# A second gate buffer for each side of an expert stage, with the residual moved to memory

## What is computed

```python
h = _rmsnorm(x, P['norm_moe_w']) * (1.0 + sc_f) + sh_f
f = _grouped_moe(h.reshape(bsz * L, D_MODEL), router_w, router_bias, ...)
x = x + g_f * f.reshape(bsz, L, D_MODEL)

def _grouped_moe(h, router_w, router_bias, w_gate, w_up, w_down):
    ...   # scores; two of 16 experts for each token; tokens sorted by expert, padded to blocks
    def expert_block(args):
        xb, e = args
        return (jax.nn.silu(xb @ w_gate[e]) * (xb @ w_up[e])) @ w_down[e]
    yb = lax.map(expert_block, (buf.reshape(n_blocks, MOE_BLOCK, D), block_expert)).reshape(n_blocks * MOE_BLOCK, D)
    return jnp.zeros_like(h).at[t_s].add(yb[pos] * w_s[:, None].astype(h.dtype))
```

## Time and profile before

| | us |
|---|---|
| median of 3 runs | 2685.18 |
| profiled execution, its own time | 2692.73 |
| span of its trace | 2690.9 |
| TensorE busy (matmul) | 2516.2 (94%) |
| VectorE busy | 1006.0 |
| ScalarE busy | 709.2 |
| mean granted TensorE clock | 0.981 |

### The profile page before, as it was taken

One profiled execution on the slowest core, in us unless ns is written; L12 is line 12 of the kernel. 1 busy time (PEld: TensorE's weight loads), 2 busy tenths in 40 slices (PEclk: granted clock), 3 DMA queues, 4 the chain that ended last, 5 costly groups with the idle time before them and its releaser, 6 DMA issues.

```text
span 2690.9 us, 39173 instructions
## 1 busy us (share of the span) xinstructions
PE 2516.2 (94%) x16348; PEld 1562.4 (58%) x16348; DVE 1006.0 (37%) x1780; ACT 709.2 (26%) x1252; POOL 66.9 (2%) x66
## 2 busy tenths in 40 slices
PE   6998999999999999999999999999997899989994
PEld 3555888885555566655555556765455444434443
DVE  4356455453223045552342548722345001101115
ACT  3132222221111111120243046731024222222224
POOL 0000000000000000000000000000000000000003
PEclk9999999999999999999999999999998999999997
DMA  7000212204000111141003011131306656657436
GB/s 313 32 32 32 75 47 106 75 31 158 32 32 31 36 52 61 58 162 71 32 18 150 32 38 40 37 118 67 109 21 268 222 209 267 238 229 286 168 135 221
DMA packets 65269, 291.99 MB, mean 109 GB/s; under 512 B 8956, under 2 KB 32068, under 8 KB 44612
## 3 DMA queue, kind: packets, MB, share of 16 engines
q1 hardware_dynamic: 52996, 255.92, 25.2%
q0 software_dynamic: 8928, 22.03, 2.4%
q10 hardware_dynamic: 3168, 11.54, 1.1%
HBM read 694.20 MB, written 56.63 MB: 279 GB/s over the span
## 4 chain that ended last, share of the span: by engine, by line
PE 79%; DMA 8%; DVE 6%; ACT 5%; issue 2%; SPq 1%; POOL 0%; DVEq 0%; ACTq 0%; POOLq 0%
PE psum L531 30%; PE psum L675 15%; PE psum L1519 8%; DMA arena<-in_moe 7%; PE psum L1377 4%; PE psum L1503 4%; PE psum L1102 3%; PE psum L630 2%; ACT arena L1758 2%; PE psum L560 1%; PE psum L1090 1%; PE psum L1015 1%; PE psum L991 1%; PE psum L1488 1%; PE psum L1082 1%
## 5 line engine op out<-in xcount | busy, mean ns | idle before, releaser
L531 PE MATMUL psum<-arena 128*128 128x384 f32 x2544 | 826.8, 487 | 10.9 <-DVEq L330 6.1
L531 PEld LDWEIGHTS psum<-arena 128*128 128x128 f32 x2544 | 483.0, 190 | 352.9 <-issue 10.5
L675 PE MATMUL psum<-arena 128*128 128x384 f32 (+1 forms) x1920 | 541.0, 427 | 6.4 <-ACT arena L689 3.3
L675 PEld LDWEIGHTS psum<-arena 128*128 128x128 f32 x1920 | 341.6, 193 | 155.1 <-issue 6.8
L1519 PE MATMUL psum<-arena 128*32 128x256 f32 x5632 | 325.7, 387 | 31.6 <-DMA arena<-in_moe 30.4
L1519 PEld LDWEIGHTS psum<-arena 128*32 128x32 f32 x5632 | 178.5, 112 | 164.8 <-DMA arena<-in_moe 37.6
L1503 PE MATMUL psum<-arena 128*32 128x512 f32 x1408 | 160.8, 594 | 10.1 <-DMA arena<-in_moe 9.5
L1927 ACT ACTIVATE arena<-psum 32x512 f32<-32x512 f32 x176 | 103.6, 589 | 226.6 <-PE psum L1503 225.0
L1377 PE MATMUL psum<-arena 128*128 128x512 f32 (+1 forms) x384 | 126.0, 487 | 0.3 <-issue 0.3
L2614 DVE TENSOR_TENSOR arena<-arena,psum 128x256 f32<-128x256 f32 x44 | 18.5, 421 | 278.0 <-PE psum L1519 188.1
L689 ACT ACTIVATE arena<-psum 128x384 f32<-128x384 f32 x96 | 46.7, 490 | 277.0 <-PE psum L675 216.7
(11 more groups left out here) (539 smaller groups left out, 2409.6 us busy)
## 6 DMA issues: line engine op xcount, KB each, us to landing
arena<-in_moe SPq DMA_DIRECT2D x532, 1024.0 KB
arena<-in_ada SPq DMA_DIRECT2D x12, 2048.0 KB, 8.8
gate_raw<-arena SPq DMA_DIRECT2D x96, 192.0 KB, 1.8
arena<-gate_raw SPq DMA_DIRECT2D x8, 2304.0 KB, 8.3
y_rows<-arena ACTq DMA_DIRECT2D x22, 512.0 KB
arena<-in_gate SPq DMA_DIRECT2D x5, 2048.0 KB, 8.4
arena<-in_br SPq DMA_DIRECT2D x4, 2048.0 KB, 8.1
arena<-in_qkv SPq DMA_DIRECT2D x3, 2048.0 KB, 15.1
```

The lines of the kernel that those rows point to most:

```text
L531: last = nc.tensor.matmul(pset(s)[:, n, :], w[:, kk, :], src[:, kk, n * N3:(n + 1) * N3], start=(kk == 0), stop=(kk == K - 1))
L675: last = nc.tensor.matmul(bank(6 + u % 2)[:, cols * p:cols * (p + 1)], w[:, m % 4, kk, :], HT[:, kk, n * N3 + cols * p:n * N3 + cols * (p ...
```

## The change

- Each side gets two gate buffers, `gset[i][0]` and `gset[i][1]`, used in even and odd steps. One lies where the gates lay in `wset[i]`, the other where the residual lies (R0 and R0 + 4096).
- The gates of step j + 2 are asked for in iteration j (`gates_ahead`), after the ups of step j + 1 and before the downs of step j. A gate part is one DMA of 2 MB instead of two halves. Whether it is loaded is told by a second table `eint2`, which compares block j with block j − 2. VectorE makes it with two small operations.
- TensorE waits for a step's gates once, on `e_wg[j % 2]`, instead of once for each half.
- The residual is stored in memory (`x_kept`) by nine DMAs of 512 KB in the routing stage (`keep_rows`), in pieces of 128 words. The gates of step 1 are asked for when all nine have landed. After the last gate products nine DMAs bring the rows back to the same place (`x_back`), token by token, and VectorE reads them there.

```diff
+        gset = [[cut(0, 4096), cut(R0, 4096)], [cut(WSET, 4096), cut(R0 + 4096, 4096)]]
+        x_back = [cut(R0 + D * s, D) for s in range(NT)]
...
+            def keep_rows(c0, c1):
+
+                for c in range(c0, c1):
+                    sp.wait_ge(m_htok, 2 * NT + 1 + 2 * (c + 1))
+                    sp.dma_start(x_kept[c * P:(c + 1) * P].rearrange("p (k f) -> p k f", k=KD),
+                                 X[:, :, c * P:(c + 1) * P]).then_inc(s_pstate, 16)
+
+            keep_rows(0, 3)
             sp.wait_ge(m_route, ROUTE_E0)
...
-            for at, done in ((0, e_wg), (4096, e_wu)):
-                for q in range(2):
-                    a = at + 2048 * q
-                    sp.dma_start(wset[1][:, a:a + 2048], first[1][:, a:a + 2048]).then_inc(done[q], 16)
+            sp.dma_start(gset[1][0], first[1][:, 0:4096]).then_inc(e_wg[0], 16)
+            for q in range(2):
+                a = 4096 + 2048 * q
+                sp.dma_start(wset[1][:, a:a + 2048], first[1][:, a:a + 2048]).then_inc(e_wu[q], 16)
+            keep_rows(3, 6)
...
             sp.dma_start(gate_p, grow[0:1].to_broadcast([P, D])).then_inc(m_grow, 16)
+            keep_rows(6, NT)
             sp.wait_ge(m_route, ROUTE_TAB)
+            sp.wait_ge(s_pstate, STATES + 16 * NT)
+            for i in range(2):
+                sp.dma_start(gset[i][1], part_expert(1, i)[:, 0:4096]).then_inc(e_wg[1], 16)
+
+            def gates_ahead(j):
+
+                sp.wait_ge(e_g, 2 * (j - 1))
+                for i in range(2):
+                    at = NST * i + j
+                    e, differs = part_expert(j, i), sp.value_load(eint2[:, at:at + 1], min_val=0, max_val=1)
+                    sp.dma_start(gset[i][j % 2], e[:, 0:4096], cond=(differs > 0)).then_inc(e_wg[j % 2], 16)
...
-                    for at, used, done in ((0, e_g, e_wg), (4096, e_u, e_wu)):
-                        for q in range(2):
-                            sp.wait_ge(used, 2 * j + q + 1)
-                            for i in range(2):
-                                a = at + 2048 * q
-                                sp.dma_start(wset[i][:, a:a + 2048], then[0][i][:, a:a + 2048], cond=(then[1][i] > 0)).then_inc(done[q], 16)
-                if 1 <= j < NST:
+                    for q in range(2):
+                        sp.wait_ge(e_u, 2 * j + q + 1)
+                        for i in range(2):
+                            a = 4096 + 2048 * q
+                            sp.dma_start(wset[i][:, a:a + 2048], then[0][i][:, a:a + 2048], cond=(then[1][i] > 0)).then_inc(e_wu[q], 16)
+                if j + 2 < NST:
+                    gates_ahead(j + 2)
+                if 1 <= j:
                     for q in range(2):
                         sp.wait_ge(e_d, 2 * (j - 1) + q + 1)
...
+            sp.wait_ge(e_g, 2 * NST)
+            for s, c in enumerate(CHUNKS):
+                sp.dma_start(x_back[s], x_kept[c * P:(c + 1) * P]).then_inc(e_wg[0 if s < 4 else 1], 16)
...
-                        pe.wait_ge(ready[q], 32 * (j + 1) + 16)
+                        if w:
+                            pe.wait_ge(e_wu[q], 32 * (j + 1) + 16)
+                        elif q == 0:
+                            pe.wait_ge(e_wg[j % 2], 32 * (j // 2 + 1) + (0 if j % 2 else 16))
...
+            V.then(tt(erow2[:, 2:NB], erow[:, 0, 2:NB], erow[:, 0, 0:NB - 2], ALU.not_equal))
+            V.then(nc.vector.tensor_copy(eint2[:, 2:NB], erow2[:, 2:NB]))
...
-                    xc = X[:, :, c * P:(c + 1) * P]
+                    xc = hd(x_back[s], KD)
```

31 lines of the change are left out of this document (19 added, 12 removed).

## The result

The changed kernel took 2730.19 us, the median of 4 runs from 2721.71 to 2733.17. The kernel before took 2687.45 us beside it, also the median of 4. The ratio is 1.0153, 95% interval 1.0123 to 1.0182: slower, by more than was forecast, and 4 us outside the range.

A forecast was written before the change was run, and what follows sets the result against it. TensorE carried 79% of what ended last, with 44.5 us lost at expert changes. Start 18.5, stage 4 and end 1 gave +23.5: profiled about 2716, less 7.5, predicted 2709 us; range 2688 to 2726, with 62% on 2698 to 2722.

The forecast's parts named there:

- With the single changes: +4: Expert stage: net 13 us saved at single expert changes and 17 lost at dense ones, together 4 us slower.
- the dense changes: Steps 14/15, 19/20, 23/24 and 27/28, expert changes close together: lose 45.4 us against 28.2 before, +17.
- down waits of 5 to 7: Steps 15, 20 and 28: TensorE waits 5 to 7 us for down parts, right behind 2 MB gate transfers.
- The start: Up to step 1: residual stores and both sides' gates delay it to about 2110; +18.5 us, bounds +12 and +22.
- The residual is the trouble: Rival: residual stores and reloads hold the first and last gather, +22 and +3; total 2714, no chance given.
- The end: After the last down product: nine residual reloads run beside the last scatter and first gathers; +1 us, bounds 0 and +3.
- The base: Profiled run taken as 7.5 us above the median of three, 2685.2, so about 2716 became 2709.
- SP kept up: SP's order in the expert stage: four more value loads and moves per iteration, some 2.3 us, would not delay it.
- The bytes: SP's queue: some 32 MB more for gates and 9.4 for the residual.
- Parts overtake: Rival: later transfers pass gates 21 in the queue, downs come in time, only the start is paid; 2668 us, 6%.
- A cheap run: Rival: parts at 0.429 take 4.9 us, stage −7, start at its low end, +12; 2691 us, 17%.
- A slow queue: Rival: long bursts at 356 GB/s, 5.9 us a part, stage +22 and start 18.5; 2726 us, 15%.

The follow-up runs named there:

- single copy: Changed kernel with the second table comparing each block with the one before, so an expert's gates load into one buffer only (some steps compute wrongly): 2697.68 us, ratio 1.0029.
- kept busy: Changed kernel with products of the identity into an unused bank where TensorE waits, at steps 1, 15, 20, 23, 24 and 28: 2727.71 us, ratio 1.0137.
- gate tables early: Changed kernel with SP's value loads for the gates two steps ahead made before its wait for the ups, transfer order unchanged: 2723.49 us, ratio 1.0125.
- gate halves: Changed kernel with each gate part in two 1 MB transfers, first halves of both sides first, and a wait for each half: 2727.03 us, ratio 1.0131.
- no trip: Changed kernel without residual stores and reloads, step 1's gates asked for once the residual is written (output lacks the residual): 2712.88 us, ratio 1.0081.
- the trip alone: Kernel before plus the residual's nine stores and nine reloads, single gate buffer, no wait for the stores before the reload: 2704.05 us, ratio 1.0055.
- Early back: Changed kernel with the nine residual reloads asked for ahead of the last two downs instead of behind them: 2724.93 us, ratio 1.0127.

## Why the forecast was right in direction and too small

**The step that failed** is "With the single changes: +4", the term of the stage, which came out at +15.3, and within it the sum for the dense changes, 45.4 forecast against 53.3 measured, and for the rest, 3.3 against 6.9. The mechanism was as described: more parts in one queue, the downs behind gates not yet needed, down waits of 5.61 at step 20, 5.54 at 28, 2.56 and 0.95 at 15; the single copy shows that the second copies cost 30.5 us where everything else in the stage won 15.1. One sign missed: at 15 down waits of 5 to 7 were forecast. The size was 11.3 us off, and it goes as follows. Step 5 loses 2.0: its gates stand behind the loads for the sample gates, which hold SP until 2139.04 and which the working left out. Steps 8 and 9 lose 1.2 more than worked out. The slow products behind a wait at 20 and 28 make 2.1 to 3.7, by the run that kept TensorE busy; the working took down products at 3.43 us wherever they stood. At 19/20 TensorE in fact waits 8.7 us, less than the 10.5 of the forecast; the other 4.8 of the 13.5 are products that take longer than undisturbed ones, and kept busy shows that most of this time would have been waited for the next part anyway.

The last 4 us or more are with the queue: 2.5 more at 14/15, 1.3 and 1.2 at 19/20 and 27/28 (more if the slow products cost less), 0.8 less at 23/24. Over two steps it was not its rate: the four rows after the change give 399/0.98, 351/0.87, 367/0.89 and 359/0.88, that is 403 to 412 GB/s of full engines, as assumed. Late asking and whole parts don't explain it either (gate tables early and gate halves). Within a burst the working was too quick. Ups 19 and gates 20, 6.3 MB asked for from 2328.85 on, would have had their first byte at 2330.05, their last at 2345.8 and their landing at 2346.9, and step 20 began at 2349.07. The table by stretch and the DMA view of 2330 to 2347 (queue q1 is SP's: packets, MB, share) say where the 2.2 us are:

```profile
2330.00:2347.00 17.00, 16.00 (x208) 7.16 (x200) 2.83 (x5) 5.04 (x9) 1.97 (x2) 1.00 0.97 381
```

```profile
q1 hardware_dynamic: 574, 6.30, 94.2%
```

SP's queue needed until 2347 for 6.30 MB, 1.2 us more than at 0.40 MB/us, and the step began 2.1 us after that, not 1.1. Why the landing comes later in a full queue was not isolated, and stays open.

**The start** was forecast at +18.5 and is +17.7, step 1 at 2110 and 2108.45. The total is right partly by luck. Two causes stand in one sum: by its terms the trip is some 14 us (10 for six stores, 4 for the round trip) and the second copy 5.5 (2.1 MB at 0.379). Of the 16.5 us measured from step 0 on, the trip has 7.8 (no trip) or 7.0 (the trip alone), and the second copy with its whole parts 8.7: one term too dear, the other too cheap. That SP is held while it issues stores into the full queue, and asks for step 1's gates later for it even where it need not wait (the trip alone), the prediction did not have. *The residual is the trouble* (+22 and +3) did not come at the start, and its end was too low.

**The end** was +1 with bounds 0 and 3, and is +4.4. The reloads did not only overlap the gathers' tail; the last scatter on the chain took 8.80 instead of 3.92. Early back returns 2.8.

**The base.** The prediction took the profiled run of before as 7.5 above the median of its three runs, and took this off. The changed kernel's profiled run lies at its own median. So 21.2 us of error are 13.9 of the terms and 7.3 of this step, which three runs do not support.

**The rest.** SP kept up, as said, in that the waits at the dense places did not go with its value loads; yet it asks for gates 9.6 and 11.4 us into step 18 and not at 9.0 and 10.3, and asking earlier was worth 4.3 us, which the prediction had at nothing. The bytes were right: 43.0 MB more on SP's queue, 41 forecast. *Parts overtake* fell: no down landed ahead of gates asked for earlier, and the down waits stayed. *A cheap run* fell with every term. *A slow queue* gave 2726, the nearest number, by a mechanism that the rows don't show: full engines moved 403 to 412 GB/s, not 356. The rule named beside it, a share of some 358 GB/s for a core (the Trainium skill, DMA: Bandwidth & Descriptors, Specifications), does not bind here: 399 GB/s over 34.7 us at 14/15. The other rule, in the same section of the Trainium skill, is line rate from 512 bytes up. Two stretches hold residual stores alone, the first with nothing ahead of them in the queue:

```profile
2048.00:2053.00 5.00, 3.04 (x24) 2.13 (x24) 4.10 (x13) 1.68 (x3) 0.00 (x0) 0.87 0.92 285
2090.50:2094.50 4.00, 0.00 (x0) 0.00 (x0) 0.00 (x0) 0.00 (x0) 0.00 (x0) 0.50 0.88 267
```

That is 310 and 303 GB/s of full engines, near the 316 of the earlier trace rows and well under the 403 to 412 of the weights, so that the measurement speaks against the rule. The trip's cost at the start, 7.0 to 7.8 us, would fit the rule's 7.3 for six stores too; it is the rate in these rows that decides.

## What to carry to other kernels

A second buffer does not only ask earlier: where parity picks the buffer, each change is loaded twice, so count bytes in the densest stretch before counting the waits that go. One queue in order turns a transfer that is needed later into lateness of one that is needed now, and moving requests about in it (four ways here, between 7 us worse and 4 us better in the stage) wins little while the bytes stay. Take a profiled run's offset from a median only if enough runs support it.

## What the runs showed of the hardware that was not expected

SP is held while it issues stores of 512-byte pieces into a full queue. The first three stores of 512 KB went into a queue with nothing else in it, the other six behind weights (duration of the issue, ns min/median/max, first and last start us):

```profile
L899 SPq DMA_DIRECT2D x_kept<-arena x3: 513/558/592, 2046.6 to 2049.2; - x3
L899 SPq DMA_DIRECT2D x_kept<-arena x6: 518/4269/9325, 2057.6 to 2087.0; - x6
```

The first three landed 3.6 to 4.5 us after issue (the stores of `h_rows` of the same size 2.6), the six 8.4 to 17.4. Three of the six took 13.1 us of SP's time to issue, and three more 13.8; everything behind them on SP waits as long. It isn't peculiar to small pieces: a 1 MB weight load at 2072.06, in the same full queue, held SP 2.6 us.

TensorE's down products behind the waits of 3.07 and 5.61 us in step 20 took 6.43 us at a granted clock of 0.56, mostly the lower of its two levels (1.2 and 2.4 GHz), against 3.64 at 1.00:

```profile
2363.50:2369.93 6.43, 6.43 (x33) 1.65 (x34) 0.00 (x0) 0.00 (x0) 0.00 (x0) 0.56 0.27 70
```

With the waits filled by other products the clock of the two steps was 1.00 instead of 0.86. A wait costs more here than its own length, unless the next part is late anyway.
